# A hybrid decoder trunk on one core: the order of the first loads, of ScalarE's first roundings, and the count of idle products before them

## The reference, cut to what matters

```python
# layer 0 (even): stick-breaking attention (8 heads) beside gated linear attention (4 heads)
h = rmsnorm(x, ln_even)
z = h @ w_in_even                      # 2048 x 7184: q, k, v, gates of both groups, gate rank 16
o_a = stick_breaking_attention(...);  y_a = o_a * silu(sb_g)
log_f = log_sigmoid(ga @ alpha_up + alpha_bias) / 16
o_b = gla_chunked(gq, gk, gv, log_f);  y_b = rmsnorm(o_b, gla_norm) * silu(gg)
x = x + concat([y_a, y_b]) @ w_out_even
# layer 1 (odd): multi-head latent attention (16 heads), low-rank q and kv, rotary key
q_lat, kv_lat, k_rope, gate = split(rmsnorm(x, ln_odd) @ w_in_odd)
o = mla_attention(rmsnorm(q_lat) @ w_q_up, rmsnorm(kv_lat) @ w_kv_up, rope(k_rope))
x = x + (o * silu(gate)) @ w_out_odd
return rmsnorm(x, final_norm)
```

## Time and profile before

| | us |
|---|---|
| median of 3 runs | 807.15 |
| lowest and highest of them | 806.45, 807.23 |
| the profiled execution, its own time | 807.16 |
| its span (first to last instruction of the program) | 805.3 |
| TensorE busy in the span | 795.3 (99%) |

### The profile page before, as it was taken

One profiled execution on the slowest core, in us unless ns is written; L12 is line 12 of the kernel. 1 busy time (PEld: TensorE's weight loads), 2 busy tenths in 40 slices (PEclk: granted clock), 3 DMA queues, 4 the chain that ended last, 5 costly groups with the idle time before them and its releaser, 6 DMA issues.

```text
span 805.3 us, 11742 instructions
## 1 busy us (share of the span) xinstructions
PE 795.3 (99%) x4138; PEld 680.7 (85%) x4138; DVE 463.8 (58%) x673; ACT 410.9 (51%) x614; POOL 126.3 (16%) x215
## 2 busy tenths in 40 slices
PE   9999999999999999999999999999999999999996
PEld 7888888888888888888888888888899999978885
DVE  5566666655554454557445645455666667754554
ACT  6753544445455454564445645335556555544452
POOL 7411132112011030230000010050000000000222
PEclk9999999999999999999999999999999999999999
DMA  9874666656657666644567666566554454435612
GB/s 315 285 220 132 183 165 172 184 161 180 176 166 198 177 198 183 204 136 144 196 196 200 179 185 195 154 196 180 164 156 138 120 181 156 153 112 169 200 55 105
DMA packets 78141, 140.30 MB, mean 174 GB/s; under 512 B 9096, under 2 KB 14384, under 8 KB 77968
## 3 DMA queue, kind: packets, MB, share of 16 engines
q1 hardware_dynamic: 76496, 137.34, 57.2%
q10 hardware_dynamic: 1440, 1.84, 0.7%
q0 software_dynamic: 160, 0.52, 0.2%
HBM read 137.06 MB, written 2.62 MB: 173 GB/s over the span
## 4 chain that ended last, share of the span: by engine, by line
PE 98%; issue 1%; DVE 0%; ACT 0%; POOLq 0%; POOL 0%; ACTq 0%; DVEq 0%
PE ps L1331 24%; PE ps L1333 24%; PE ps L1332 24%; PE ps L1716 2%; PE ps L1715 2%; PE ps L1717 2%; PE ps L1353 2%; PE ps L1798 1%; PE ps L1758 1%; PE ps L1757 1%; PE ps L1759 1%; PE ps L1514 1%; PE ps L1388 1%; PE ps L1467 1%; PE ps L1769 1%
## 5 line engine op out<-in xcount | busy, mean ns | idle before, releaser
L930 DVE TENSOR_TENSOR w_lo<-raw,w_hi 128x1024 fp32r<-128x1024 f32 x239 | 302.7, 1268 | 285.8 <-ACT w_hi L607 285.2
L607 ACT ACTIVATE w_hi<-raw 128x1024 fp32r<-128x1024 f32 x236 | 249.8, 1059 | 295.5 <-PE ps L1333 280.3
L1331 PE MATMUL ps<-w_hi,a_hi 128*128 128x512 f32 x868 | 341.6, 394 | 0.2 <-issue 0.2
L1333 PE MATMUL ps<-w_hi,a_lo 128*128 128x512 f32 x868 | 338.2, 390 | 0.0
L1332 PE MATMUL ps<-w_lo,a_hi 128*128 128x512 f32 x868 | 337.9, 389 | 0.0
L1333 PEld LDWEIGHTS ps<-w_hi,a_lo 128*128 128x128 f32 x868 | 162.9, 188 | 34.4
L1331 PEld LDWEIGHTS ps<-w_hi,a_hi 128*128 128x128 f32 x868 | 163.0, 188 | 33.2 <-issue 0.6
L1332 PEld LDWEIGHTS ps<-w_lo,a_hi 128*128 128x128 f32 x868 | 163.1, 188 | 32.4
L1715 PE MATMUL ps<-a_hi,w_hi 128*128 128x256 f32 x160 | 45.8, 286 | 0.0
L1716 PE MATMUL ps<-a_hi,w_lo 128*128 128x256 f32 x160 | 45.3, 283 | 0.0
L1717 PE MATMUL ps<-a_lo,w_hi 128*128 128x256 f32 x160 | 45.3, 283 | 0.0
(11 more groups left out here) (265 smaller groups left out, 792.4 us busy)
## 6 DMA issues: line engine op xcount, KB each, us to landing
raw<-in_w_in_even SPq DMA_DIRECT2D x111, 512.0 KB, 3.8
raw<-in_w_in_odd SPq DMA_DIRECT2D x48, 512.0 KB, 3.7
raw<-in_w_out_even SPq DMA_DIRECT2D x32, 512.0 KB, 3.8
raw<-in_w_out_odd SPq DMA_DIRECT2D x32, 512.0 KB, 3.7
raw<-in_w_kv_up SPq DMA_DIRECT2D x16, 512.0 KB, 3.7
raw<-in_w_q_up SPq DMA_DIRECT2D x16, 384.0 KB, 3.3
xs<-in_x SPq DMA_DIRECT2D x6, 256.0 KB, 8.8
even<-in_final_norm SPq DMA_DIRECT2D x1, 1024.0 KB, 6.4
```

The costliest lines, as they stand in the source:

```text
L607: return a.activation(w_hi[:, ring, 0:w], raw[:, s, 0:w], ACT.Copy)
L930: return v.tensor_tensor(w_lo[:, ring, 0:w], raw[:, s, 0:w], w_hi[:, ring, 0:w].bitcast(F32), ALU.subtract)
L1331: m.matmul(acc, a_hi[:, k, tok], hi, start=first, stop=False)
L1333: ins = m.matmul(acc, a_lo[:, k, tok], hi, start=False, stop=last)
```

## The change

It touches four places of the opening.

```diff
@@ SP @@
             sp.dma_start(gain_rows, ln_even[0].rearrange("(k p) -> k p", p=P)).then_inc(first_gains_landed, 16)
+            sp.dma_start(xs[:, 1, 0:HW], x_d[1][:, 0:HW]).then_inc(x_half_landed[1], 16)
             for kk in range(PK):
                 sp.dma_start(raw[:, 0, kk * CW:kk * CW + CW], we_d[:, kk, G_QK:G_QK + CW]).then_inc(half_landed if kk == 0 else raw_landed[0], 16)
+            for t in range(T):
+                sp.dma_start(xs[:, t, HW:CW], x_d[t][:, HW:CW]).then_inc(x_landed[t], 16)
             first_piece(1)
@@ ScalarE @@
-            for half in range(2):
-                for t in range(T):
-                    cols = slice(HW * half, HW * half + HW)
-                    act.dma_start(xs[:, t, cols], x_d[t][:, cols]).then_inc(x_landed[t] if half else x_half_landed[t], 16)
+            act.dma_start(xs[:, 0, 0:HW], x_d[0][:, 0:HW]).then_inc(x_half_landed[0], 16)
             a.preload_act_table_set("natural_log_exp_and_others")
             x_prep = prep(steps_from(U_PREP0), 0)
+            act.wait_ge(gain_ready, 1)
+            act.wait_ge(t_done, 1)
+            a.activation(a_hi[:, 0, :], ps[:, 4, 0:256], ACT.Copy, scale=gain_t[:, 0:1]).then_inc(first_hi, 1)
             act.wait_ge(half_landed, 16)
             a.activation(w_hi[:, 0, 0:CW], raw[:, 0, 0:CW], ACT.Copy).then_inc(half_hi, 1)
-            act.wait_ge(gain_ready, 1)
-            act.wait_ge(t_done, 1)
-            for kk in range(2):
-                a.activation(a_hi[:, kk, :], ps[:, 4, 256 * kk:256 * kk + 256], ACT.Copy,
-                             scale=gain_t[:, kk:kk + 1]).then_inc(t_free_a if kk else first_hi, 1)
+            a.activation(a_hi[:, 1, :], ps[:, 4, 256:512], ACT.Copy, scale=gain_t[:, 1:2]).then_inc(t_free_a, 1)
@@ TensorE @@
-            idle_products(11)
+            idle_products(6)
...
             transpose_step(U_PREP0, 0, xs, (0,))
-            idle_products(3)
+            idle_products(2)
```

## The result

The changed kernel took 808.39 us (median of 22 runs, 807.81 to 809.23), the kernel before beside it 807.10 (22 runs, 806.45 to 807.62): ratio 1.0017, 95% interval 1.0011 to 1.0024. It is slower by 1.3 us. That is less than the 0.2% (1.6 us) of the prediction, but the interval tells it from no change, and it lies outside the range, which ended at 807.8.

What follows compares the result with a forecast made beforehand. TensorE, busy 795.3 of 805.3 us, was taken as the bound. The first product's 1.5 us gain, less 0.6 (quarter of x), 0.2 (norms' rows) and 0.25 (`gates_up`), left 0.45: 806.7 us, range 806.0 to 807.8.

Steps and rivals of the forecast that it cites:

- First product: TensorE's first real product in the opening: starts at 6.1 in place of 7.63, 1.5 us earlier.
- Rival 4: Opening: x's tile 1 half or first weights land as late as before, first product 7.0 to 7.6; 806.8 to 807.15; chance 0.08.
- rival 3: TensorE's clock rises later in the opening, through piece 0: 806.9, or 808.0 (0.85 slower); chance 0.13.
- Rival 1: Transfers' stream comes earlier through a shorter slow start: 0.75 to 1.5 us gained, 805.7 to 806.4; chance 0.13.
- (a): TensorE waits for x's second quarter, landing at 10.25: of the 1.5 us gained, 0.9 is kept.
- (b): TensorE at the next norms' rows, taken to land at 20.7: start no earlier than 20.75, 0.7 us kept.
- (c): `gates_up` in block 1, limited by a chain from block 1's first piece: 42.35 instead of 42.80, 0.45 us kept.
- The stream: Delivery of all transfers from x's second quarter on: bounds 1.35 us later to 0.3 earlier, taken as 0.
- The cover: SP's three extra issues ahead of piece 1, 1.35 us, are hidden while the engines are behind the issues.
- Rival 2: Stream later, from SP's queue ahead of piece 1: one queue with 1 KB rows slower, or issues unhidden; 0.9 slower; chance 0.16.

Runs made afterwards that it cites:

- e4: Kernel before with three small transfers (16 rows of 256 B each) issued on SP's queue ahead of piece 1; 807.32 us.
- e1: Kernel before with only the three transfers of x moved to SP's queue, roundings' order and idle products as before; 807.84 us.
- e5: Changed kernel with block 1's first four pieces issued ahead of the bias, the six copies and the gla norm's row; 807.40 us.
- e15: Changed kernel with eleven idle products instead of six; 807.74 us.
- e17: Changed kernel unaltered, run and profiled again; 808.57 us.
- e18: e5 with eleven idle products instead of six; 807.85 us.
- e7: Kernel before with queues exchanged: x's four transfers on SP's ahead of piece 1, piece 0's halves on ScalarE's; 807.00 us.
- e10: Changed kernel with the second half of piece 0 on ScalarE's queue; 808.19 us.
- e12: Changed kernel with block 1's first four pieces issued early, as in e5, and piece 1 on ScalarE's queue; 809.42 us.
- e13: e10 with eleven idle products instead of six; 807.76 us.
- e2: Changed kernel with x's four transfers back on ScalarE's queue; new roundings' order and 6 + 2 idle products remain; 808.37 us.
- e9: e10 with block 1's first four pieces issued early, as in e5; 807.98 us.
- e11: e3 with block 1's first four pieces issued early, as in e5; 808.00 us.
- e3: Changed kernel with x's second halves on ScalarE's queue; 807.80 us.

## Why the prediction was wrong

**First product, clock in the opening.** Right: 6.04 for 6.1, the gain row's transpose at 3.98 (3.7 to 3.8 forecast), the higher level reached between 3.4 and 4.6. Rival 4 and, for the first profile, rival 3 are out.

Rival 1's shorter slow start did come, 233 GB/s for 179 from 2 to 4 us, and was lost again by 8 us.

**The chain (a), (b), (c).** Its links held. TensorE did wait for x's quarter, the norms' rows and `gates_up`, in this order, and (c) was the right last limit: the 0.45 that the prediction let it keep is the 42.80 of before less 29.86 + 12.47. What went into the chain was wrong.

**The stream: the failed step.** "Bounds: 1.35 later to 0.3 earlier ... I take 0." Measured, the quarter came 1.76 late, piece 6 2.34 late (22.34 for 20.00), the issue of block 1's first piece 2.77 and its landing 2.58; from the usual run's span (806.7) `gates_up` is at 44.2, which puts that landing at no later than 31.7. The cover I named did hold for block 1's landing: with SP's issues 1.4 us later it moved by 0.1 (e4). What I had not asked is whether the engines, busy at 0.93 and 0.87 of their time instead of 1.07 and 1.04, move as much per busy microsecond: 257 and 249 GB/s for 387 and 368. I had read the share of busy time as a rate. Before, ScalarE's queue with x's four transfers was a second feed beside the first weights. With only one of them left there, the sixteen shares of piece 1 landed from 7.48 to 9.83 (7.58 to 8.42 before), and everything behind them in the one queue kept that spread: x's quarter from 9.41 to 11.98. In the six profiles of kernels with x's first half alone on ScalarE's queue (changed, e1, e5, e15, e17, e18) 2.00 to 2.24 MB had moved by 10 us, at no more than 304 GB/s from 6 to 8 us and 287 from 8 to 10; in the fourteen with more on it, 2.23 to 2.50 MB, at no less than 308 and 301. The closest pair is e1 and e4: piece 1 is issued at 3.61 and 3.59, and block 1's piece landed at 31.18 and 29.94. That a second loaded queue keeps the rate is what these groups, e7 and e10 show, by different amounts. Why a single one falls behind is not settled: the spread of the shares is no mark of it, as the quarter's shares lay 2.5 us apart in e12 and 2.6 in e13 too. Nor was one queue tried with piece 1 issued as early as before, so how much the late issue adds when there is no second queue is open.

The Trainium skill, "DMA: Bandwidth & Descriptors", section "Issuing engines are not separate DMA queues", grants a second issuing engine nothing but the issue time. Here the issue time alone moved block 1's landing by 0.1 us (e4), and against the changed kernel's 257 GB/s the second queue had 379 in e10 and 312 in e13: for these first microseconds the measurement decides against the page.

**Why it grew on the way.** SP issues in order, and the held-up issue of the bias ended at 23.65 instead of 21.61, 2.04 late; the six copies behind it took 3.48 us instead of 2.75. In the first profile one copy's issue took 1.15 us beside an instruction transfer of 16 KB at 23.87; before, one of that size fell at 19.65, inside the issue held up for 7.08, and cost nothing. Issuing block 1 ahead of the bias and the copies returned 1.0 us (e5).

**Rival 2.** Right in place and sign (808.0, chance 0.16), and half right in its first reason: one queue did feed the engines worse than two, but the 1 KB rows were not why (e7). Its second reason, the issues not hidden, fell with e4 for block 1's landing. It was too small, as its 0.9 was the bound of issue time. The mechanism was on the list, then, at a chance of 0.16, and the forecast put it at nothing. **Rival 3** was given the wrong place. The opening's clock rose in time; the risk lay in the wait that the earlier start itself creates at (a), 2.4 and 2.1 us in the two profiles instead of the half microsecond of the prediction. In e2, e9, e10, e11 and e12 the late rise is where rival 3 had it, and there it eats what the stream gives back.

**The sum as measured**, in the first profile: start 1.6 earlier, all of it and 1.0 more lost at the quarter, 0.6 at the norms' rows, 0.5 at block 1's landing: 2.1 at `gates_up`, 807.16 + 2.1 = 809.3 for a run of 809.23. In the usual run the loss is 1.3, of which block 1's landing has some 1.0 (e5). How often a fallen clock has a part in it is open.

## What to carry to other kernels

Before moving transfers from one queue to another, read GB/s and not only the busy share of the engines. In this kernel two loaded queues kept the rate up while the first pieces arrive; it paid only where the second did not carry what delays the first weights (e7 against e10 and e12). An earlier start only helps if the next transfer is earlier too; otherwise it is turned into a longer wait, and that wait may cost the clock besides. Large transfers issued in order behind small ones that nobody needs yet should go ahead of them where the buffers allow: it was worth 1.0 us in the changed kernel, and in the kernel before nothing that could be told.

## What was not expected of the hardware

- The granted clock fell to half for 3.4 us (12.6 to 16.0, weight loads of up to 337 ns instead of 187) behind a wait of 2.1 us, having risen at 5.8; in another execution a wait of 2.4 us did not do it.
- With the same first instructions the clock rose at 4.0 in one trace (e4) and at 6.0 in another (before).
- An instruction transfer of 16 KB lies beside an SP issue of 1.15 to 1.58 us in the changed kernel, e2, e3, e5 and e17; whether it is the cause was not tested.
